# Reordered mixers of a hybrid decoder trunk: halved first chunks, squares last, the third pair's output products beside the last head norm

## The reference

```python
def mixer_ab(h, w_in, w_out, ...):            # h = rms_norm(x)
    u = h @ w_in                              # columns ax, ag, r, k, v (512 each), dw, da, dg
    ax = causal_depthwise_conv(ax, conv_w, conv_b)
    ya = rg_lru(ax, ...) * gelu(ag)           # r, i = sigmoid(block-diagonal gates of ax)
    bc = bc + (prev - bc) * mu                # token shift of r, k, v, dw, da, dg
    yb = rwkv7_time_mix(bc, ...)              # decay, key norm, delta-rule scan, head norm, bonus, gate
    return concatenate([ya, yb]) @ w_out
```

## Time and profile before

| | |
|---|---|
| median of 3 runs | 1609.93 us (1607.43 to 1612.05) |
| the profiled execution | 1612.51 us, its span 1610.7 us |
| mean granted TensorE clock | 0.967 |
| busy: PE, DVE, ACT, POOL | 94%, 51%, 30%, 5% |
| chain that ended last: PE, DVE, ACT, DMA | 85%, 6%, 4%, 3% |
| layer 0's mixers | about 0 to 410 us of the span |
| fronts p = 1 and 3 | begin at 126.4 and 301.2 us; `azb_t` at 180.5 and 355.3 us |

### The profile page before, as it was taken

The page is one execution under the profiler, slowest core; times in us unless marked ns, Lnnn a source line. Parts: engine busy times, 40 slices in busy tenths (PEclk is TensorE's granted clock), DMA queues, the critical chain, the costliest instruction groups (busy, mean ns, idle before and its releaser), DMA issues.

```text
span 1610.7 us, 22894 instructions
## 1 busy us (share of the span) xinstructions
PE 1506.7 (94%) x10312; PEld 1237.8 (77%) x10312; DVE 814.2 (51%) x991; ACT 477.5 (30%) x517; POOL 81.6 (5%) x73
## 2 busy tenths in 40 slices
PE   6779999998899999999898998999997999999996
PEld 5577777878688888888786877877876888888885
DVE  5547475664763535354654435334445745444443
ACT  4343434342432212223323123122234322221220
POOL 1000000000300000000300000000002100000001
PEclk9889999999899999999899999999997999999998
DMA  4101112020132322332131312312311233233221
GB/s 169 53 16 57 43 33 67 15 93 3 58 118 99 105 97 86 105 105 81 51 105 52 105 52 79 105 52 79 105 53 52 79 105 104 80 105 105 82 101 53
DMA packets 19297, 125.07 MB, mean 78 GB/s; under 512 B 2240, under 2 KB 2240, under 8 KB 5120
## 3 DMA queue, kind: packets, MB, share of 16 engines
q1 hardware_dynamic: 18800, 121.23, 22.1%
q0 software_dynamic: 400, 2.39, 0.4%
HBM read 121.51 MB, written 2.10 MB: 77 GB/s over the span
## 4 chain that ended last, share of the span: by engine, by line
PE 85%; DVE 6%; ACT 4%; DMA 3%; issue 1%; POOL 0%; POOLq 0%; SPq 0%; DVEq 0%
PE bank L285 22%; PE bank L291 21%; PE bank L288 21%; PE bank L548 7%; DMA raw<-weights 3%; PE bank L1121 2%; PE bank L1092 2%; PE bank L1098 2%; PE bank L1095 2%; PE bank L299 1%; DVE WL L258 1%; ACT WH L252 1%; PE bank L1113 1%; PE bank L556 1%; PE bank L563 1%
## 5 line engine op out<-in xcount | busy, mean ns | idle before, releaser
L285 PE MATMUL bank<-XH,WH 128*128 128x512 f32 x944 | 382.0, 405 | 34.5 <-DVE WL L258 19.3
L291 PE MATMUL bank<-XH,WL 128*128 128x512 f32 x944 | 374.5, 397 | 0.0
L288 PE MATMUL bank<-XL,WH 128*128 128x512 f32 x944 | 374.3, 397 | 0.0
L258 DVE TENSOR_TENSOR WL<-raw,WH 128x2048 fp32r<-128x2048 f32 (+1 forms) x113 | 254.4, 2251 | 194.0 <-ACT WH L252 194.0
L252 ACT ACTIVATE WH<-raw 128x2048 fp32r<-128x2048 f32 (+1 forms) x113 | 212.2, 1878 | 418.2 <-DMA raw<-weights 418.1
L285 PEld LDWEIGHTS bank<-XH,WH 128*128 128x128 f32 x944 | 181.8, 193 | 77.2 <-issue 34.6
L291 PEld LDWEIGHTS bank<-XH,WL 128*128 128x128 f32 x944 | 181.1, 192 | 39.4
L288 PEld LDWEIGHTS bank<-XL,WH 128*128 128x128 f32 x944 | 181.8, 193 | 38.4 <-issue 1.4
L285 PE MATMUL bank<-AH,WH 128*128 128x512 f32 x512 | 199.4, 389 | 0.0
L291 PE MATMUL bank<-AH,WL 128*128 128x512 f32 x512 | 199.2, 389 | 0.0
L288 PE MATMUL bank<-AL,WH 128*128 128x512 f32 x512 | 199.2, 389 | 0.0
(11 more groups left out here) (255 smaller groups left out, 1655.8 us busy)
## 6 DMA issues: line engine op xcount, KB each, us to landing
raw<-weights SPq DMA_DIRECT2D x109, 1024.0 KB, 4.8
h<-x_fm SPq DMA_DIRECT2D x4, 512.0 KB, 7.4
raw<-weights SPq DMA_DIRECT2D x4, 512.0 KB, 3.8
out_fm<-h SPq DMA_DIRECT2D x8, 256.0 KB, 2.0
rc<-ret_const POOLq DMA_DIRECT2D x1, 1536.0 KB, 6.8
pp<-pairs POOLq DMA_DIRECT2D x4, 199.0 KB, 4.0
cst<-const SPq DMA_DIRECT2D x1, 577.0 KB, 10.4
vec<-vectors SPq DMA_DIRECT2D x1, 41.5 KB, 1.9
```

The source lines that it names most:

```text
L258: nc.vector.tensor_tensor(WL[i][:, :n], raw[i][:, :n], WH[i][:, :n], ALU.subtract).then_inc(S("w_lo"), 1)
L285: mm = pe.matmul(bank[b][:], wh, xh, start=(k == 0), stop=False)
L288: mm = pe.matmul(bank[b][:], wh, xl, start=False, stop=False)
L291: mm = pe.matmul(bank[b][:], wl, xh, start=False, stop=(k == len(xs) - 1))
```

## The change

The start: chunks 0 and 1 are fetched, copied and subtracted in halves; SP's queue is x0, first half of chunk 0, x1, second half, x2, x3, both halves of chunk 1, then the constants (before: x0, x1, chunk 0, x2, x3, constants, chunk 1). ACT makes all `XH` first and the squares afterwards; DVE does the small steps of `sp` before the sums of squares. A one-element Sigmoid stands before the Tanh of `lora`, and PE's low ranks no longer wait for `gate_in`. Only 2 of `k`'s 8 tiles stand ahead of the spread.

The fronts: PE's order is `k`, `r`, `ax`, `rk_sum`, `lin_g`, `v`, gates, `ag`, outputs; in pair 0 also, where `r` now uses bank 7. The splits of chunks 4p+4 and 4p+5 move: ACT's behind `ya_hi` and behind the last copy of `chunks_act`, DVE's first one behind the mask `O`. DVE's adds alternate with its steps of the LRU. Pair 2's outputs leave front 3 and go to front 4, between the head norm's products, in banks 1, 0, 3, 4. The split of chunk 18 goes behind the squares of the last outputs; `chunk_left` for chunk 16 is now raised at pair 3's outputs, so chunk 18 is fetched from there, where it was fetched from the start of `chunks_pe(3)`.

```diff
+        def first_half_hi(act, c):
+            act.wait_ge(S(f"half_loaded{c}"), 16)
+            nc.scalar.activation(WH[c][:, :CHUNK // 2], raw[c][:, :CHUNK // 2], ACT.Copy).then_inc(S("half_hi"), 1)
...
-                return 2 if name == "k" else 3
-            return 1 if name in ("r", "ax") else 0
+                return 2 if name == "k" else 7
+            return 1 if name in ("r", "v") else 0
...
-            return m % 4 if pair == PAIRS - 1 else (m + 1) % 2
+            return m % 4 if pair == LAST else (1, 0, 3, 4)[m % 4] if pair == LAST - 1 else (m + 1) % 2
...
-            if pair == PAIRS - 1:
-                units(pe, use, range(4), ws[:4], ys, 0, y_tile(pe, pair))
-            for m in range(4 if pair == PAIRS - 1 else 0, KT):
-                units(pe, use, [out_bank(m, pair)], [ws[m]], ys, 1 if m == 0 else 0, y_tile(pe, pair) if m == 0 else None)
+            if pair == LAST:
+                units(pe, use, range(4), ws[:4], ys, 1, y_tile(pe, pair))
+            for m in ms:
+                if pair < LAST or m >= 4:
+                    units(pe, use, [out_bank(m, pair)], [ws[m]], ys, 1 if m == 0 and pair < LAST - 1 else 0,
+                          y_tile(pe, pair) if m == 0 else None)
...
+            if p == PAIRS:
+                out_units(pe, use, LAST - 1, (0,))
+                was("ys")
+                pe.matmul(bank[5][:], heads, Zt[:], start=True, stop=True).then_inc(S("y_sum"), 1)
+                out_units(pe, use, LAST - 1, (1, 2))
+                was("yc_sq")
+                head_sums(pe, 6, ARK, "y_var")
+                out_units(pe, use, LAST - 1, (3, 4))
+                was("ln_inv")
+                head_spread(pe, 7, lninv, "ln_spread")
+                out_units(pe, use, LAST - 1, (5, 6, 7))
+                out_units(pe, use, LAST)
+                return
...
+                pe.wait_ge(S("half_lo"), 2)
+                in_unit(pe, use, "k", 0, (0, 2))
                 pe.wait_ge(S("const_loaded"), 16)
                 pre_spread_pe(pe, 0)
-                in_unit(pe, use, "r", 0)
-                in_unit(pe, use, "v", 0)
-                pe.wait_ge(S("lora_ready"), 2)
-                pe.wait_ge(S("acc_free2"), use.now(2))
-                pe.wait_ge(S("acc_free3"), use.now(3))
+                in_unit(pe, use, "k", 0, (2, 4))
+                chunk_ready(pe, 1)
+                in_unit(pe, use, "k", 0, (4, KT))
+                pe.wait_ge(S("lora_ready"), 1)
...
-            if p < PAIRS:
-                need("rk_ready")
-                if p:
-                    was("yn")
-                pe.matmul(bank[7][:], heads, W[3][:], start=True, stop=True).then_inc(S("rk_sum"), 1)
-                pe.matmul(bank[2][:], pp[p % 2][:, P_G2:P_G2 + P], gate_in[:], start=True, stop=True).then_inc(S("lin_g"), 1)
-                if p:
-                    in_unit(pe, use, "ax", p)
-                in_unit(pe, use, "ag", p)
-                need("lru_in", "decay_rate", "iclr")
-                pe.wait_ge(S("gate_blocks"), 4 * p + 4)
-                pe.matmul(bank[3][:], BDa[:], lax[:], start=True, stop=True).then_inc(S("gate_r"), 1)
-                pe.matmul(bank[4][:], BDx[:], lax[:], start=True, stop=True).then_inc(S("gate_i"), 1)
+            in_unit(pe, use, "r", p, (0, 4))
+            need("kk_sq")
+            head_sums(pe, 6, W[7], "kk_sum")
+            in_unit(pe, use, "r", p, (4, KT))
+            need("kk_inv")
             if p:
+                was("yc")
+            head_spread(pe, 5, kkinv, "kk_spread")
+            in_unit(pe, use, "ax", p)
+            need("rk_ready")
+            if p:
+                was("yn")
+            pe.matmul(bank[7][:], heads, W[3][:], start=True, stop=True).then_inc(S("rk_sum"), 1)
+            pe.wait_ge(S("lora_ready"), 2)
+            pe.matmul(bank[2][:], pp[p % 2][:, P_G2:P_G2 + P], gate_in[:], start=True, stop=True).then_inc(S("lin_g"), 1)
+            in_unit(pe, use, "v", p)
+            need("lru_in", "decay_rate", "iclr")
+            pe.wait_ge(S("gate_blocks"), 4 * p + 4)
+            pe.matmul(bank[3][:], BDa[:], lax[:], start=True, stop=True).then_inc(S("gate_r"), 1)
+            pe.matmul(bank[4][:], BDx[:], lax[:], start=True, stop=True).then_inc(S("gate_i"), 1)
+            in_unit(pe, use, "ag", p)
+            if 0 < p < LAST:
                 out_units(pe, use, p - 1)
...
-                split_hi(act, 4 * p + 4)
...
-                need("lru_iu")
+                need("lru_scale")
                 nc.scalar.activation(Uag[:], Uag[:], ACT.Gelu_apprx_tanh).then_inc(S("gelu"), 1)
-                split_hi(act, 4 * p + 5)
                 need("ya_ready")
                 nc.scalar.activation(yH[p % 2][:, 0, :], Bt[:], ACT.Copy).then_inc(S("ya_hi"), 1)
+                split_hi(act, 4 * p + 4)
...
-            if p == PAIRS - 1:
-                split_hi(act, FFN0_CHUNK + 1)
+            split_hi(act, 4 * p + 5)
...
+                last = [out_bank(m, LAST - 1) for m in range(KT)]
+                for m in range(KT):
+                    add_to_f(dve, use, last[m], m, False)
+                    if m == 0:
+                        head_centred()
+                    if m == 2:
+                        head_inverse()
+                    if m == 3:
+                        normalized()
+                        yb_low()
                 return
...
-            in_evac(dve, use, "ag", p)
+            split_lo(dve, 4 * p + 3)
+            in_evac(dve, use, "v", p)
+            need("b_ready")
+            shift_mix(dve, p, "v")
+            need("rk_sum", "v_mixed")
+            nc.vector.tensor_tensor(bonus[:], W[2][:], bank[7][:], ALU.mult).then_inc(S("bonus"), 1)
             need("lru_i", "lru_in")
             nc.vector.tensor_tensor(Bt[:], Bt[:], lax[:], ALU.mult).then_inc(S("lru_iu"), 1)
-            if p:
-                for m in range(4):
-                    add_to_f(dve, use, out_bank(m, p - 1), m, p == 1)
+            in_evac(dve, use, "ag", p)
+            out = 0 < p < LAST
             need("lru_a", "lru_root")
             nc.vector.scalar_tensor_tensor(Kt[:], ARB[:], 1.0, Kt[:], ALU.add, ALU.mult).then_inc(S("lru_scale"), 1)
+            if out:
+                adds(0)
             need("lru_scale", "lru_iu")
             nc.vector.tensor_tensor(Kt[:], Kt[:], Bt[:], ALU.mult).then_inc(S("lru_drive"), 1)
-            split_lo(dve, 4 * p + 4)
-            if p:
-                for m in range(4, 6):
-                    add_to_f(dve, use, out_bank(m, p - 1), m, p == 1)
+            if out:
+                adds(1)
             need("lru_drive")
             nc.vector.tensor_tensor_scan(Bt[:], ARB[:], Kt[:], 0.0, ALU.mult, ALU.add).then_inc(S("lru_h"), 1)
+            if out:
+                adds(2)
             need("lru_h", "gelu")
             nc.vector.tensor_tensor(Bt[:], Bt[:], Uag[:], ALU.mult).then_inc(S("ya_ready"), 1)
-            if p:
-                for m in range(6, 8):
-                    add_to_f(dve, use, out_bank(m, p - 1), m, p == 1)
+            if out:
+                adds(3)
             need("ya_hi", "ya_ready")
             nc.vector.tensor_tensor(yL[p % 2][:, 0, :], Bt[:], yH[p % 2][:, 0, :], ALU.subtract).then_inc(S("ya_lo"), 1)
+            if out:
+                adds(4, 5, 6, 7)
...
             masked(O, 6, K_O, "azb", "o")
+            split_lo(dve, 4 * p + 4)
...
-                square_f(act, 0, m, use, out_bank(m, PAIRS - 1))
+                square_f(act, 0, m, use, out_bank(m, LAST))
+            split_hi(act, FFN0_CHUNK + 1)
...
+            H = CHUNK // 2
             for j in range(4):
                 sync.dma_start(h[:, 2 * j:2 * j + 2, :], x[j * 2 * P:(j + 1) * 2 * P, :].rearrange("(k p) t -> p k t", p=P)
                                ).then_inc(S(f"x_loaded{j}"), 16)
+                if j == 0:
+                    sync.dma_start(raw[0][:, :H], weights[0][:, :H]).then_inc(S("half_loaded0"), 16)
                 if j == 1:
-                    sync.dma_start(raw[0][:], weights[0]).then_inc(S("raw_loaded0"), 16)
+                    sync.dma_start(raw[0][:, H:], weights[0][:, H:]).then_inc(S("raw_loaded0"), 16)
+            sync.dma_start(raw[1][:, :H], weights[1][:, :H]).then_inc(S("half_loaded1"), 16)
+            sync.dma_start(raw[1][:, H:], weights[1][:, H:]).then_inc(S("raw_loaded1"), 16)
             sync.dma_start(cst[:], const).then_inc(S("const_loaded"), 16)
-            for c in range(1, ALL_CHUNKS):
+            for c in range(2, ALL_CHUNKS):
...
+            first_high(act, (0, 1))
+            first_half_hi(act, 0)
+            first_high(act, (2, 3))
+            second_half_hi(act, 0)
+            first_high(act, (4, 5, 6, 7))
+            first_half_hi(act, 1)
+            second_half_hi(act, 1)
+            first_squares(act)
+            split_hi(act, 2)
             pre_root_act(act, 0)
             pre_copy_act(act, 0)
-            split_hi(act, 2)
```

(48 more changed lines are left out.)

69 lines of the change are left out of this document (30 added, 39 removed).

## The result

| | before | changed |
|---|---|---|
| median | 1608.70 us (4 runs, 1607.43 to 1612.05) | 1580.03 us (4 runs, 1579.72 to 1583.52) |
| the profiled execution, its span | 1612.51, 1610.7 us | 1583.52, 1581.7 us |
| mean granted clock | 0.967 | 0.972 |
| PE busy | 1506.7 us | 1501.1 us |

The account below looks back on a forecast made before the run. PE bounds the kernel, busy 1506.7 of 1610.7 us, so its pauses and low clock were the target. Gains 23.1 + 5.5 + 3.9 + 4.7 = 37.2 take the median from 1609.93 to 1572.7 us; range 1563 to 1584.

Parts of the forecast that it names:

- Start: First layer's start: first product at 9.4 us, not 14.6; squares' additions just in time; `Ur` at 27.4, 9.4 earlier.
- Rival (d): At the start, half chunks land no earlier or squares delay the sums: at most 5.2 us back, 1577.9; chance 0.05.
- Pair 0: First pair: new pauses of 3.1 before key sums and `m2`, 1.6 for half pace; 23.1 us gained including the start.
- the 2.2 of half pace: Behind pair 0's second pause, 96 products took 5.17 against 2.97 us; excess left unchanged in the forecast, may vanish.
- Pairs 1 and 2: Middle pairs: outputs no longer wait for ACT's root or banks; gains of 5.5 and 3.9 us.
- Rival (c): In pairs 1 and 2 output tiles still wait for DVE's chain or ACT's root: 9.4 us lost, 1582.1; chance 0.06.
- The moved split: DVE's split of 2.29 us behind `O` costs nothing, fitting 2.45 idle; without cover up to 2.3 a pair.
- Pair 3 and the last outputs: Last pair gains 11.8 us without output products; the last norm, taking them, ends 7.1 later: net 4.7.
- rival (a): Every new pause, and the 2.2 one, is followed by 3.8 us lost: 9.8 more, 1582.5; chance 0.14.
- (b): No half pace after any pause: 1.6 + 1.6 + 2.2 us less, 1567.3; chance 0.10.
- (e): Half pace, once entered, stays through the pairs' units: 67 us lost, 30 net, slower at 1640; chance 0.02.
- (f): Each table switch holds ACT for twice its 1.28 us: 8.5 more in all, 1581.2; chance 0.01.

Follow-up runs that it names:

- sums_on_dve: Against the changed kernel: DVE makes all six additions of the first norm's squares, POOL none; 1579.19 us, ratio 0.9808 to the kernel before.
- steps_behind: Against the changed kernel: DVE's small steps of `sp` go back behind the first norm's reciprocal; 1579.72 us, ratio 0.9794 to the kernel before.
- whole_chunks: Against the changed kernel: chunks 0 and 1 are fetched, copied and subtracted whole again; 1582.02 us, ratio 0.9824 to the kernel before.
- ag_before_gates: Against the changed kernel: in pairs 1 and 2 the gate products stand behind `ag` again; 1592.57 us, ratio 0.9898 to the kernel before.
- outs_in_front3: Against the changed kernel: pair 2's outputs go back to front 3, in banks 1 and 0; 1582.30 us, ratio 0.9825 to the kernel before.
- again: The changed kernel itself, run once more with nothing altered; 1582.91 us, ratio 0.9825 to the kernel before.

## Why the prediction was right or wrong

**Start: wrong in one step.** First product 10.11 for 9.4, since the half chunk was copied from 7.58, not 6.9; the 48 products took 13.5 for 13.4. The failed step is "the additions behind them end at 22.5 to 22.7: just in time". It walked ACT's squares and priced the additions as if DVE stood ready, and left out the 15 small steps that the change puts in front of them: 6.2 us, six of them 4.36 beside POOL. The sums came at 26.79, 4.0 late, and `Ur` at 32.90, 5.5 late: the other 1.5 is PE's slow clock after the new pause (0.73 in its window). Rival (d) named the sums as the weak place, but by late squares, at 5.2 us; the squares were done at 21.2 as forecast. It has the right size and the wrong mechanism. The 4 us have two parts. In `sums_on_dve`, with the steps in front but POOL silent, the 15 steps take 3.0 and DVE's first three additions end at 23.6: the order alone makes them 0.9 later than the forecast's 22.7, contention the other 3.1. Nor is 27.4 reached by the order of before: in `steps_behind` `Ur` stands at 29.00.

**Pair 0: right shape.** One pause of 2.55 before the key sums (forecast 3.1), unbroken work from there to `ag`'s end at 70.87 (27.9, the forecast's 24.6 and half pace), one pause before `m2` (2.98 for 3.1), the reload before Tanh gone. From key sums to `m2` lie 34.8, forecast 33.1: half pace took 3 here where I wrote 1.6. In `whole_chunks` the same stretch took 31.9 (42.34 to 74.20) with the key sums at full pace: the price of a pause of 2 to 3 us ran from nothing to 3 us between executions. In return the 2.2 of half pace that I left behind `m2` vanished here. That is luck, and the prediction named it only as something that may happen: 5.5 at the start and 1.7 here, less these 2.2, make the pair 5.0 worse than forecast (4.8 on the table).

**Pairs 1 and 2: right,** 5.5 and 4.3 for 5.5 and 3.9, and the reason given holds: `ag_before_gates` takes the gain away through the waits for root and bank that the walk named. Rival (c) falls. The moved split cost nothing.

**Pair 3 and the last outputs.** The two terms came out at 11.7 for 11.8 and 8.45 for 7.1; the pause for add 6's bank was 2.00, forecast 2.2. The mis-sized term is the last one: 48 products took 12.8 us at a clock of 0.87, not 11.4 (at full pace they take 10.9). That is half pace behind the new pause, as rival (a) has it, but 1.9 us of it and not 3.8; the sums behind them lost 0.65 more. What the forecast did not see is how the 4.7 net divides: `outs_in_front3` shows that the move itself brings nothing, and that the gain of pair 3 comes from the order inside the pair: 82.7 us there, against 87.8 before.

**The other rivals.** (a) and (b) were posed as "every pause" and "none"; the truth is some of each. (e) did not occur: every low stretch ended within the window after its pause. (f) falls: the added load took 1.28 and the activation stood 0.02 behind it. Tanh followed at 35.14 with no load, so "at every change of function" says too much:

```profile
32.83 1.28 ACT L1412 ACT_TABLE_LOAD   x1
34.13 0.20 ACT L1412 ACTIVATE epsc<-epsc 128x1 f32<-128x1 f32 x1
35.14 0.63 ACT L1414 ACTIVATE lora<-lora 64x512 f32<-64x512 f32 x1 [0.81 <-DVE lora L1484]
```

What stays open is what decides whether a given pause is followed by half pace; no experiment here set it.

## What to carry to other kernels

When a step is moved, price it at its new place: what runs on the other engines at that moment, and what is queued behind it. "Just in time" on one engine's walk needs the queue of the engine that consumes as well. The trace of the kernel before may hold the price already, as it did here for DVE beside POOL. Work moved under a dependent chain pays only if its buffers do not come back through that same chain; count the banks before counting the products.

## What the runs showed of the hardware

- A DVE step on 128x4 that takes 0.16 us alone took up to 1.287 us beside a POOL addition of 128x512, about as long as that addition (1.29). DVE additions of 128x512 took 1.54 each beside POOL (3.08 for two), 0.69 to 0.75 alone. In `whole_chunks`, where other small steps fell beside POOL's three additions, three were slowed by 1.0 to 1.1 us each, TENSOR_SCALAR with its one input too, which took 1.27 and 1.21 instead of 0.17. In the trace before, two instructions for `XL` took 1.02 and 1.09 more than their 0.75. The price is not a share of the instruction's own work: for each POOL addition it was 1.0 to 1.1 us on steps of 0.16, about as much on `XL`, and 0.8 on the additions.
- Equal pauses are followed by different paces. After 2.97 to 2.98 us of idle time before `m2`, the 96 products took 3.01 in pair 0 and 4.30 in pair 3 of one execution, 3.01 and 3.02 in `again`. In the traces of the changed kernel and the ten runs such a pause stands 21 times: behind 11 of them the 96 products took 3.01 or 3.02, behind the other 10 they took 4.25 to 5.38, as in `ag_before_gates`:

```profile
79.64 5.38 PE L575 MATMUL bank<-W,W 64*64 64x64 f32 x96 [2.98 <-DVE W L1027]
```

With five pauses of 2 to 3 us in these mixers and up to 3 us behind each, this is as large as the spread of a kernel's runs here (3 to 9 us).
